# Second pointwise projection of a Conformer module, from fp32 matmuls to three products of rounded parts

## The chip, the cores and the metric

The kernel runs on one core of a Trainium2 chip. The metric is the device time of one execution in microseconds; the median of several executions is compared. The engines are TensorE (PE: matmuls; PEld: its weight loads), VectorE (DVE), ScalarE (ACT), GpSimd (POOL) and SyncE (SP), which issues most DMAs.

## The reference

A two-layer trunk over x of 256 tokens and 1024 channels, in float32. Layer 0 is a Conformer convolution module and a dense SwiGLU, layer 1 a windowed attention and a top-2-of-8 expert SwiGLU. The change lies in the convolution module:

```python
def conformer_conv_module(h, pw1_w, pw1_b, dw_w, dw_b, ln_g, ln_b, pw2_w, pw2_b):
    u = h @ pw1_w + pw1_b
    a, gate = jnp.split(u, 2, axis=-1)
    u = a * jax.nn.sigmoid(gate)
    u = lax.conv_general_dilated(u, dw_w[:, None, :], window_strides=(1,), padding=[(CONV_WIDTH - 1, 0)], ...) + dw_b
    u = jax.nn.silu(layernorm(u, ln_g, ln_b))
    return u @ pw2_w + pw2_b

x = x + conformer_conv_module(rmsnorm(x, norm_mix_g[0]), ...)
x = x + swiglu(rmsnorm(x, norm_ffn_g[0]), ffd_w_gate[0], ffd_w_up[0], ffd_w_down[0])
```

pw1_w is 1024x2048, the depthwise filter has 31 taps, pw2_w is 1024x1024.

## The kernel before

The program is written engine by engine: each engine has one instruction stream in the order of its code, and waits for semaphores that others raise. Nothing reorders the instructions. Channels stand in 8 chunks of 128 partitions (DC), tokens in two tiles of 128 (TT).

**Weights.** They come in units of 1 MB (2048 fp32 per partition) through a ring of 7 slots, which SyncE fills in order: 8 units of pw1, 4 of pw2 (U_PW2, numbers 8 to 11, each two input chunks of 1024 outputs), then 33 of the dense SwiGLU (from U_FFD, number 12), K, V, Q, the output projection and the experts. The load of unit n waits until unit n - 7 is no longer needed (L445 to L452).

**Two kinds of product.** The matmuls of pw1 (L1075), of the filter (L1095) and of pw2 (L1120) take fp32 operands as they are. From the dense SwiGLU on, each weight half-unit is split: ScalarE casts it to a rounded high part (wh, four places, L773), VectorE subtracts that from the ring's fp32 to get the low part (wl, L1611), and TensorE adds three products: high x high, high x low, low x high. Activations are split in the same manner (hTh, hTl, both in the tensor `both`).

**The convolution module.** TensorE makes pw1 in four groups of two chunks; ScalarE takes the sigmoid of each gate (L723), VectorE multiplies (L1550, the gated product). The filter is shared: VectorE makes chunks 0 to 4 and part of chunk 5 tap by tap (L1557 and 169 operations of 128x256 on L1560), TensorE the rest of 5, and 6 and 7, as 74 matmuls with diagonal matrices that ScalarE writes (L711). In VectorE's stream two gated products each stand ahead of taps number 32, 68 and 98. Then TensorE sums for mean and variance (L1085, L1106), VectorE normalizes (L1601, L1603), ScalarE applies Silu (L760) into the fp32 tensor sq, and TensorE multiplies by pw2 (L1120): tile 0, then tile 1, and for each of 8 chunks two halves of 512 outputs. After four chunks of tile 1 it transposes the updated X of tile 0 (L1021). The bias pw2_b is added to X by VectorE ahead of its first gated product (L1545), and the projection when a tile is done (add_mix, L1520). ScalarE and VectorE then write the high and low parts of the scaled X of each tile (L784, L1640), with which the dense SwiGLU begins (L1184, L1186).

GpSimd has little to do ahead of the attention: constants, powers for the norms, and the DMAs of biases and small parameters (L555 to L562).

## Time and profile before

| | |
|---|---|
| median of 3 runs | 1395.81 us (1395.0 to 1400.91) |
| profiled execution | 1393.66 us, span 1391.9 us |
| PE busy | 1370.0 us (98%) |
| DVE busy | 1178.7 us (85%) |
| ACT busy | 985.6 us (71%) |
| POOL busy | 93.3 us (7%) |
| mean granted TensorE clock | 0.997 |
| bytes moved | 428.97 MB, mean 308 GB/s |

Times in the profile count from the start of the span. Consecutive instructions of one kind are merged in the timelines: the first number is the start, the second the time from the start of the first to the end of the last, xN the count; square brackets hold the engine's idle time before the row and what ended it. Two successive instructions of one engine overlap a little in the records, so the pace is read from starts. An fp32 matmul leaves two records: the 32 instructions of L1120 show as x64. "R" stands for any of the buffers R1, R2 and R3.

### The profile page before, as it was taken

How to read it: one execution, taken by the hardware profiler on the slowest of the kernel's cores; microseconds unless marked ns; L12 is line 12 of the kernel's file. 1: busy time of each engine (PE TensorE's matmuls, PEld its weight loads, DVE VectorE, ACT ScalarE, POOL GpSimd, SP SyncE). 2: the span in 40 equal slices, each digit the busy share in tenths (PEclk: the TensorE clock that was granted, in tenths of full speed). 3: DMA queues.
4: the chain of work that ended last, by engine and by line, in shares of the span. 5: the costliest groups of instructions: out<-in, count | busy, mean ns of one | idle time of the engine just before them, and what ended most of it. 6: DMA issues, size and time to landing. Idle time of an engine off the chain costs nothing.

```text
span 1391.9 us, 20466 instructions
## 1 busy us (share of the span) xinstructions
PE 1370.0 (98%) x6699; PEld 1136.2 (82%) x6699; DVE 1178.7 (85%) x1391; ACT 985.6 (71%) x1249; POOL 93.3 (7%) x121
## 2 busy tenths in 40 slices
PE   9999999999999999999999999999999999999997
PEld 8885888888887888888888888888888888888885
DVE  3993666667768998999999899999989999999997
ACT  3174544455667788877878887787888788778885
POOL 1000000002224000000000000000000000000000
PEclk9999999999999999999999999999999999999999
DMA  9602665555637999999999999999999999999992
GB/s 293 228 24 79 205 195 187 186 198 166 197 103 289 395 396 367 395 395 374 359 394 395 337 394 394 354 376 394 393 332 394 396 353 379 395 384 342 395 394 104
DMA packets 197230, 428.97 MB, mean 308 GB/s; under 512 B 7263, under 2 KB 44255, under 8 KB 197182
## 3 DMA queue, kind: packets, MB, share of 16 engines
q1 hardware_dynamic: 192510, 412.79, 81.0%
q0 software_dynamic: 4512, 15.51, 4.0%
q8 instruction: 28, 0.46, 0.1%
q14 instruction: 20, 0.16, 0.0%
q10 hardware_dynamic: 160, 0.04, 0.0%
HBM read 419.67 MB, written 8.65 MB: 308 GB/s over the span
## 4 chain that ended last, share of the span: by engine, by line
PE 91%; DVE 4%; ACT 3%; issue 1%; ACTq 0%; DVEq 0%; POOL 0%; POOLq 0%
PE bank L1135 70%; PE bank L1184 6%; PE bank L1075 4%; PE bank L1186 3%; PE bank L1095 2%; PE bank L1120 2%; PE bank L1424 2%; DVE wl L1611 2%; ACT wh L773 1%; PE bank L1001 1%; ACT prob L853 0%; ACT both L916 0%; PE bank L1106 0%; PE bank L1332 0%; PE bank L1085 0%
## 5 line engine op out<-in xcount | busy, mean ns | idle before, releaser
L1611 DVE TENSOR_TENSOR wl<-ring,wh 128x1024 fp32r<-128x1024 f32 x758 | 907.9, 1224 | 70.7 <-ACT wh L773 25.7
L773 ACT CAST wh<-ring 128x1024 fp32r<-128x1024 f32 x758 | 789.3, 1055 | 167.5 <-PE bank L1135 167.5
L1135 PE MATMUL bank<-wh,both 128*128 128x512 f32 (+1 forms) x1888 | 583.5, 391 | 0.9 <-DVE wl L1611 0.7
L1135 PEld LDWEIGHTS bank<-wh,both 128*128 128x128 f32 x1888 | 349.0, 188 | 72.3 <-DVE wl L1611 2.8
L1135 PE MATMUL bank<-wl,both 128*128 128x512 f32 (+1 forms) x944 | 366.4, 388 | 0.0
L1135 PEld LDWEIGHTS bank<-wl,both 128*128 128x128 f32 x944 | 177.2, 188 | 37.1
L1135 PE MATMUL bank<-wh,ath 128*128 128x512 f32 x512 | 201.2, 393 | 0.9
L1135 PE MATMUL bank<-wl,ath 128*128 128x512 f32 x512 | 199.6, 390 | 0.0
L1135 PE MATMUL bank<-wh,atl 128*128 128x512 f32 x512 | 199.3, 389 | 0.0
L1184 PE MATMUL bank<-both,wh 128*128 128x512 f32 x352 | 124.8, 399 | 1.4 <-DVE both L1640 1.1
L1135 PEld LDWEIGHTS bank<-wh,ath 128*128 128x128 f32 x512 | 96.1, 188 | 23.5 <-DVE wl L1611 3.8
L1135 PEld LDWEIGHTS bank<-wl,ath 128*128 128x128 f32 x512 | 96.1, 188 | 20.6
L1135 PEld LDWEIGHTS bank<-wh,atl 128*128 128x128 f32 x512 | 96.2, 188 | 19.4
L1186 PE MATMUL bank<-both,wl 128*128 128x256 f32 x352 | 98.7, 280 | 0.0
L1184 PEld LDWEIGHTS bank<-both,wh 128*128 128x128 f32 x352 | 66.1, 188 | 18.1 <-DVE both L1640 1.4
L1560 DVE SCALAR_TENSOR_TENSOR R<-R 128x256 f32<-128x256 f32 x169 | 67.5, 500 | 0.0
L1186 PEld LDWEIGHTS bank<-both,wl 128*128 128x128 f32 x352 | 66.4, 189 | 0.4
L1075 PE MATMUL bank<-R,ring 128*128 128x256 f32 x256 | 55.8, 380 | 0.1
L1075 PEld LDWEIGHTS bank<-R,ring 128*128 128x128 f32 x256 | 48.5, 190 | 7.1 <-issue 0.6
L1890 DVE TENSOR_TENSOR atl<-bank,ath 128x512 fp32r<-128x512 f32 x56 | 38.4, 686 | 10.5 <-ACT ath L931 10.5
L931 ACT CAST ath<-bank 128x512 fp32r<-128x512 f32 x56 | 32.4, 579 | 16.8 <-PE bank L1424 16.8
L1897 DVE TENSOR_TENSOR R<-bank,R 128x512 f32<-128x512 f32 x56 | 38.3, 685 | 1.8 <-PE bank L1135 1.8
(251 smaller groups left out, 892.0 us busy)
## 6 DMA issues: line engine op xcount, KB each, us to landing
ring<-in_moe_w_gate SPq DMA_DIRECT2D x112, 1024.0 KB, 7.4
ring<-in_moe_w_up SPq DMA_DIRECT2D x112, 1024.0 KB, 7.7
ring<-in_moe_w_down SPq DMA_DIRECT2D x112, 1024.0 KB, 7.8
ring<-in_conv_pw_w SPq DMA_DIRECT2D x12, 1024.0 KB, 10.9
ring<-in_ffd_w_gate SPq DMA_DIRECT2D x11, 1024.0 KB, 5.3
ring<-in_ffd_w_up SPq DMA_DIRECT2D x11, 1024.0 KB, 5.5
ring<-in_ffd_w_down SPq DMA_DIRECT2D x11, 1024.0 KB, 5.0
ring<-in_w_q SPq DMA_DIRECT2D x4, 1024.0 KB, 4.9
```

What stands on the lines that cost most here:

```text
L773: sa.copy(wh[:, place(n, h), :], ring_half(n, h)).then_inc(wh_ready, 1)
L931: sa.copy(ath[:, :, :], PB[2][:, :].rearrange("p (j s) -> p j s", j=4)).then_inc(ath_ready, 1)
L1075: mm = pe.matmul(PB[2 * g + j % 2][:, c * S:(c + 1) * S], w[:, k, c * P:(c + 1) * P], hT[:, k, :], start=(k == 0), stop=(k == DC - 1))
L1095: mm = pe.matmul(PB[4 + c - DVE_CHUNKS][:, 0:S], taps[:, m % DIAGS, :], upad[:, c, w:w + S], start=(w == 0), stop=(w == last_tap))
L1120: mm = pe.matmul(x_bank(t, half)[:, :], tokens(sq[:, k, :], t), w[:, k % 2, half * HALF:(half + 1) * HALF], start=(k == 0), stop=(k == DC ...
L1135: mm = pe.matmul(out_bank, lhs, rhs, start=start and n == 0, stop=stop and n == 2, **kw)
L1184: pe.matmul(banks[c][:, :], wide, hTb[:, k, :, :].rearrange("p a s -> p (a s)"), start=(k == 0), stop=False)
L1186: mm = pe.matmul(banks[c][:, 0:S], narrow, hTh[:, k, :], start=False, stop=(k == DC - 1))
L1560: ins = ve.scalar_tensor_tensor(out=v, in0=upad[:, c, w:w + S], scalar=dw[:, c, w:w + 1], in1=v, op0=ALU.mult, op1=ALU.add)
L1611: ve.tensor_tensor(wl[:, place(n, h), :], ring_half(n, h), wh[:, place(n, h), :].bitcast(F32), ALU.subtract).then_inc(wl_ready, 1)
L1890: ve.tensor_tensor(atl[:, :, :], PB[2][:, :].rearrange("p (j s) -> p j s", j=4), ath[:, :, :].bitcast(F32), ALU.subtract).then_inc(atl_rea ...
L1897: ve.tensor_tensor(act, PB[1][:, :], act, ALU.mult).then_inc(act_ready, 1)
```

## The change

1. The second projection is made of three products of rounded parts. The eight half-units of pw2 get high parts (mix_high: the four places of wh, and hnl, yh and yl, which have no other use until much later) and low parts (mix_low: the four places of wl, and qh and ql).
2. ScalarE casts the high parts behind the sigmoids of chunks 3 and 5, four each. GpSimd subtracts for the low parts, each when its high part is ready.
3. ScalarE applies Silu twice, once into the rounded hTh and once into the fp32 sq; VectorE's mix_lows subtract, to hTl.
4. SyncE reloads the ring slots of pw2 when the low parts exist, no longer when the matmuls are done. The first four feed-forward casts wait for the chunks of tile 1 that still use their places.
5. The bias pw2_b is added to X by GpSimd instead of VectorE.
6. VectorE's small preparations (router weights, sinks) and the first feed-forward low parts stand behind the mix_lows and the addition of tile 0 to X.

```diff
--- before.py
+++ after.py
@@ -180,6 +180,10 @@
         hTb = both[:, CHUNK:CHUNK + 2 * DC * S].rearrange("p (k a s) -> p k a s", k=DC, a=2)
         hTh, hTl = hTb[:, :, 0, :], hTb[:, :, 1, :]
 
+        mix_high = [wh[:, k, :] for k in range(SPLITS)] + [hnl[:, 0, :], hnl[:, 1, :], yh[:, :], yl[:, :]]
+        mix_low = [wl[:, k, :] for k in range(SPLITS)] + [q.rearrange("p (c k) s -> p c (k s)", c=2)[:, c, :]
+                                                          for q in (qh, ql) for c in range(2)]
+
         upad = R2[:, :].rearrange("p (k s) -> p k s", k=DC)
         sq = R2[:, 0:2048].rearrange("p (k s) -> p k s", k=DC)
         dw = R3[:, 2816:3072].rearrange("p (k w) -> p k w", k=DC)
@@ -295,6 +299,10 @@
         std_ready = sem("std_ready")
         vn_ready = sem("vn_ready")
         s_ready = sem("s_ready")
+        s_high = sem("s_high")
+        s_low = sem("s_low")
+        mix_high_ready = sem("mix_high_ready")
+        mix_low_ready = sem("mix_low_ready")
         tile_done = sem("tile_done")
         x_upd = sem("x_upd")
         dve = sem("dve_chain")
@@ -445,7 +453,9 @@
             def load(n, src, k):
                 if n >= RING:
 
-                    if n - RING < U_FFD:
+                    if U_PW2 <= n - RING < U_FFD:
+                        sp.wait_ge(mix_low_ready, 2 * (n - RING - U_PW2 + 1))
+                    elif n - RING < U_FFD:
                         sp.wait_ge(units_used, n - RING + 1)
                     else:
                         split_done(sp, n - RING, 1)
@@ -562,6 +572,16 @@
             pool.dma_start(scratch, spread(small[0:HEADS, 0:DELTAS].rearrange("h (a d) -> h a d", a=1), 1, CHUNK))\
                 .then_inc(bias_out, 16)
 
+            pool.wait_ge(pw2b_in, 16)
+            pool.wait_ge(xT_done, 4)
+            for t in range(TT):
+                pool.tensor_tensor(X[:, t, :], X[:, t, :], pw2_bias, ALU.add).then_inc(x_biased, 1)
+
+            for k in range(DC):
+                pool.wait_ge(mix_high_ready, k + 1)
+                pool.tensor_tensor(mix_low[k], ring_half(U_PW2 + k // 2, k % 2), mix_high[k].bitcast(F32),
+                                   ALU.subtract).then_inc(mix_low_ready, 1)
+
             for t in range(TT):
                 root(1, t)
 
@@ -722,6 +742,12 @@
                     sa.wait_ge(glu_ready, c - 1)
                 sa.activation(sig[:, c % 2, :], PB[2 + c // 2 % 2][:, (c % 2) * S:(c % 2 + 1) * S], ACT.Sigmoid,
                               bias=cv[:, CV_PW1B + DC + c:CV_PW1B + DC + c + 1]).then_inc(sig_ready, 1)
+                if c in (3, 5):
+
+                    for k in range(2 * c - 6, 2 * c - 2):
+                        if k % 2 == 0:
+                            landed(sa, U_PW2 + k // 2)
+                        sa.copy(mix_high[k], ring_half(U_PW2 + k // 2, k % 2)).then_inc(mix_high_ready, 1)
 
             def taps_to(c):
 
@@ -757,9 +783,9 @@
                 for c in range(DC):
 
                     sa.wait_ge(vn_ready, 2 * t + (1 if c < DVE_CHUNKS else 2))
-                    sa.activation(tokens(sq[:, c, :], t), tokens(v_chunk(c), t), ACT.Silu,
-                                  bias=cv[:, CV_LNB + c:CV_LNB + c + 1],
-                                  scale=cv[:, CV_LNG + c:CV_LNG + c + 1]).then_inc(s_ready, 1)
+                    norm = dict(bias=cv[:, CV_LNB + c:CV_LNB + c + 1], scale=cv[:, CV_LNG + c:CV_LNG + c + 1])
+                    sa.activation(tokens(hTh[:, c, :], t), tokens(v_chunk(c), t), ACT.Silu, **norm).then_inc(s_high, 1)
+                    sa.activation(tokens(sq[:, c, :], t), tokens(v_chunk(c), t), ACT.Silu, **norm).then_inc(s_ready, 1)
 
 
             def high_parts(n, later=0):
@@ -768,6 +794,9 @@
                     if n >= U_MOE or half_no(n, h) >= SPLITS:
 
                         sa.wait_ge(halves_used, later * PASS_HALVES + (half_no(n, h) - SPLITS + 1))
+                    elif h == 0:
+
+                        sa.wait_ge(units_used, U_PW2 + half_no(n, h) // 2 + 1)
                     if h == 0:
                         landed(sa, n, later)
                     sa.copy(wh[:, place(n, h), :], ring_half(n, h)).then_inc(wh_ready, 1)
@@ -1112,14 +1141,17 @@
                 for k in range(DC):
                     if t == 1 and k == 4:
                         raw_T(1, 0, xT_first)
-                    if t == 0 and k % 2 == 0:
-                        landed(pe, U_PW2 + k // 2)
-                    pe.wait_ge(s_ready, DC * t + k + 1)
-                    w = slot(U_PW2 + k // 2).rearrange("p (k f) -> p k f", k=2)
-                    for half in range(2):
-                        mm = pe.matmul(x_bank(t, half)[:, :], tokens(sq[:, k, :], t),
-                                       w[:, k % 2, half * HALF:(half + 1) * HALF], start=(k == 0),
-                                       stop=(k == DC - 1))
+                    if t == 0:
+                        pe.wait_ge(mix_low_ready, k + 1)
+                    pe.wait_ge(s_high, DC * t + k + 1)
+                    for a, w in ((hTh, mix_high[k]), (hTh, mix_low[k]), (hTl, mix_high[k])):
+                        if a is hTl:
+                            pe.wait_ge(s_low, DC * t + k + 1)
+                        for half in range(2):
+                            mm = pe.matmul(x_bank(t, half)[:, :], tokens(a[:, k, :], t),
+                                           w[:, half * HALF:(half + 1) * HALF],
+                                           start=(k == 0 and a is hTh and w is mix_high[k]),
+                                           stop=(k == DC - 1 and a is hTl))
                     if t == TT - 1 and k % 2:
                         consume(mm)
                 if t == 0:
@@ -1539,10 +1571,6 @@
             ve.wait_ge(bias_row_done, 1)
             ve.tensor_copy(bias_rows, PB[1][0:HEADS, 0:DELTAS]).then_inc(bias_row, 1)
 
-            ve.wait_ge(pw2b_in, 16)
-            ve.wait_ge(xT_done, 4)
-            for t in range(TT):
-                ve.tensor_tensor(X[:, t, :], X[:, t, :], pw2_bias, ALU.add).then_inc(x_biased, 1)
             ve.wait_ge(cv_ready, 2)
 
             def glu(c):
@@ -1623,6 +1651,17 @@
                                             in1=high_part[:, k, :].bitcast(F32), op0=ALU.mult,
                                             op1=ALU.subtract).then_inc(h_low, 1)
 
+            def mix_lows(t, chunks):
+
+                for c in chunks:
+                    ve.wait_ge(s_ready, DC * t + c + 1)
+                    ve.tensor_tensor(tokens(hTl[:, c, :], t), tokens(sq[:, c, :], t),
+                                     tokens(hTh[:, c, :], t).bitcast(F32), ALU.subtract).then_inc(s_low, 1)
+
+            mix_lows(0, range(DC))
+            mix_lows(1, range(DC))
+            ve.wait_ge(x_biased, 2)
+            add_mix(1, 0)
             ve.wait_ge(router_in, 32)
             ve.tensor_tensor(rw[:, :, :], rw[:, :, :],
                              spread(cv[:, CV_FFN1:CV_FFN1 + DC].rearrange("p (k a) -> p k a", a=1), 2, E),
@@ -1631,7 +1670,6 @@
             ve.tensor_scalar(nsinks[:, :], sinks[:, :], -1.0, None, ALU.mult).then_inc(nsinks_ready, 1)
             low_parts(dense_at["g", 0])
             low_parts(dense_at["u", 0])
-            ve.wait_ge(x_biased, 2)
             def norm_low_tile(t):
                 for k in range(DC):
                     if k % 2 == 0:
@@ -1642,7 +1680,6 @@
                                             in1=tokens(hTh[:, k, :], t).bitcast(F32), op0=ALU.mult,
                                             op1=ALU.subtract).then_inc(h_low, 1)
 
-            add_mix(1, 0)
             mean_square(1, 0)
             scale_diag(1, 0)
             norm_low_tile(0)
```

TensorE at the second projection, before (ring is the fp32 weight slot, R the activations sq):

```order
L1001 MATMUL bank<-ident 128x128 x10
L1120 MATMUL bank<-ring,R 128x512 x24
L1021 MATMUL bank<-ident,X 128x128 x8
L1120 MATMUL bank<-ring,R 128x512 x8
L1001 MATMUL bank<-ident 128x128 x2
L1021 MATMUL bank<-ident,X 128x128 x8
```

The same place now: the first chunks of tile 0, the transposes within tile 1, the end of tile 1 (L1151 is the projection; wl, qh and ql hold low parts of weights, wh, hnl, yh and yl high ones):

```order
L1030 MATMUL bank<-ident 128x128 x10
L1151 MATMUL bank<-wh,both 128x512 x2
L1151 MATMUL bank<-wl,both 128x512 x2
L1151 MATMUL bank<-wh,both 128x512 x4
L1151 MATMUL bank<-wl,both 128x512 x2
...
L1151 MATMUL bank<-wl,both 128x512 x2
L1151 MATMUL bank<-wh,both 128x512 x2
L1050 MATMUL bank<-ident,X 128x128 x8
L1151 MATMUL bank<-hnl,both 128x512 x2
...
L1151 MATMUL bank<-ql,both 128x512 x2
L1151 MATMUL bank<-yl,both 128x512 x2
L1030 MATMUL bank<-ident 128x128 x2
L1050 MATMUL bank<-ident,X 128x128 x8
```

Each fp32 matmul gives way to three on parts, 96 in all; the transposes keep their place after four chunks of tile 1.

GpSimd between its early DMAs and the LayerNorm, before:

```order
L559 DMA gB<-in_norm_ffn_g 128x1024
L562 DMA bias_scratch<-small 1024x1x192
L548 TENSOR_TENSOR rstd<-ms,mhalf 128x1 x2
L569 MEMSET ones 128x128
L548 TENSOR_TENSOR rstd<-ms,mhalf 128x1 x2
```

The same place now (L578 adds the bias, L582 makes the low parts of the eight half-units of pw2):

```order
L569 DMA gB<-in_norm_ffn_g 128x1024
L572 DMA bias_scratch<-small 1024x1x192
L578 TENSOR_TENSOR X<-X,R 128x1024 x2
L582 TENSOR_TENSOR wl<-ring,wh 128x1024 x4
L582 TENSOR_TENSOR qh<-ring,hnl 128x1024 x2
L582 TENSOR_TENSOR ql<-ring,yh 128x1024
L582 TENSOR_TENSOR ql<-ring,yl 128x1024
L558 TENSOR_TENSOR rstd<-ms,mhalf 128x1 x2
```

Ten operations of 128x1024 stand where there was none.

VectorE at the start of the filter, and behind the LayerNorm, before (L1545 adds the bias, L1603 is the last LayerNorm product, L1611 the first feed-forward low parts, L1520 the addition of tile 0):

```order
L1545 TENSOR_TENSOR X<-X,R 128x1024 x2
L1550 SCALAR_TENSOR_TENSOR R<-bank,cv,R 128x256 x2
L1557 TENSOR_SCALAR R<-R,cv 128x256 x2
L1560 SCALAR_TENSOR_TENSOR R<-R 128x256 x30
...
L1603 TENSOR_TENSOR R<-R 128x3x128
L1627 TENSOR_TENSOR rw<-rw,cv 128x64
L1631 TENSOR_SCALAR nsinks<-sinks 128x16
L1611 TENSOR_TENSOR wl<-ring,wh 128x1024 x4
L1520 TENSOR_TENSOR X<-bank,X 128x512 x2
```

The same two places now:

```order
L1578 SCALAR_TENSOR_TENSOR R<-bank,cv,R 128x256 x2
L1585 TENSOR_SCALAR R<-R,cv 128x256 x2
L1588 SCALAR_TENSOR_TENSOR R<-R 128x256 x30
...
L1631 TENSOR_TENSOR R<-R 128x3x128
L1658 TENSOR_TENSOR both<-R,both 128x128 x16
L1552 TENSOR_TENSOR X<-bank,X 128x512 x2
L1666 TENSOR_TENSOR rw<-rw,cv 128x64
L1670 TENSOR_SCALAR nsinks<-sinks 128x16
L1639 TENSOR_TENSOR wl<-ring,wh 128x1024 x4
```

The bias is gone from the head of the filter; 16 low parts of activations (L1658) and the addition of tile 0 (L1552) stand ahead of the feed-forward low parts (L1639).

## Rows read from the trace of the kernel before

**Rows 1.** The page, part 4: shares of the chain that ended last, by engine

```profile
PE 91%; DVE 4%; ACT 3%; issue 1%; ACTq 0%; DVEq 0%; POOL 0%; POOLq 0%
```

**Rows 2.** The chain in order of time, 0 to 160 us: start, length, what

```profile
66.97 30.23 PE bank L1095 x140
...
101.08 1.29 PE bank L1085 x6
...
110.63 20.84 PE bank L1120 x48
...
132.34 6.88 PE bank L1120 x16
139.25 0.70 DVE X L1520
```

**Rows 3.** Waits of the DMA queue (SPq), whole run: waited for, total us, times, longest

```profile
SPq L507 <- DVE wl L1611: 821.7, 336, 21.6
```

**Rows 4.** Timeline of VectorE, 25 to 101 us: start us, us, what, count

```profile
25.93 2.36 DVE L1545 TENSOR_TENSOR X<-X,R 128x1024 f32<-128x1024 f32 x2 [7.12 <-DMA R<-in_conv_pw_b]
...
29.76 11.98 DVE L1560 SCALAR_TENSOR_TENSOR R<-R 128x256 f32<-128x256 f32 x30
41.63 0.89 DVE L1550 SCALAR_TENSOR_TENSOR R<-bank,cv,R 128x256 f32<-128x256 f32 x2
...
69.11 0.89 DVE L1550 SCALAR_TENSOR_TENSOR R<-bank,cv,R 128x256 f32<-128x256 f32 x2
...
95.62 4.47 DVE L1560 SCALAR_TENSOR_TENSOR R<-R 128x256 f32<-128x256 f32 x11
```

**Rows 5.** Timeline of ScalarE: two of the four pairs of sigmoids

```profile
39.38 0.84 ACT L723 ACTIVATE R<-bank,cv 128x256 f32<-128x256 f32 x2 [10.64 <-PE bank L1075]
...
67.00 0.84 ACT L723 ACTIVATE R<-bank,cv 128x256 f32<-128x256 f32 x2 [12.98 <-PE bank L1075]
```

**Rows 6.** Groups by line and form, 0 to 210 us: count, busy us, mean ns, idle

```profile
L1120 PE MATMUL bank<-ring,R 128*128 128x512 f32 x64 | 27.9, 593 | 0.2 <-ACT R L760 0.2
...
L773 ACT CAST wh<-ring 128x1024 fp32r<-128x1024 f32 x26 | 25.9, 1054 | 0.0
...
L760 ACT ACTIVATE R<-R,cv 128x128 f32<-128x128 f32 x16 | 6.2, 478 | 0.0
```

**Rows 7.** Timeline of TensorE in the experts, 610 to 614 us

```profile
611.51 0.62 PE L1135 MATMUL bank<-wh,both 128*128 128x512 f32 x2
...
613.57 0.62 PE L1135 MATMUL bank<-wh,both 128*128 128x512 f32 x2
```

**Rows 8.** Timelines of ScalarE and VectorE in the second tile

```profile
126.03 1.06 ACT L685 ACTIVATE R<-X 128x1024 f32<-128x1024 f32 x1 [6.00 <-DVE X L1520]
...
128.06 0.29 DVE L1503 TENSOR_SCALAR R<-ident,rstd 128x128 f32<-128x128 f32 x1 [0.69 <-POOL rstd L548]
...
132.38 2.16 DVE L1640 SCALAR_TENSOR_TENSOR both<-bank,cv,both 128x128 fp32r<-128x128 f32 x8 [4.04 <-ACT both L784]
```

**Rows 9.** Groups by form on GpSimd, 360 to 430 us

```profile
L617 POOL TENSOR_TENSOR prob<-X,gB 128x1024 f32<-128x1024 f32 x2 | 4.8, 2403 | 12.9 <-DVE X L1520 12.9
```

**Rows 10.** Timelines from 419 us (GpSimd, VectorE); by tile: ns min/median/max

```profile
419.89 7.54 POOL L633 TENSOR_SCALAR prob<-prob,rstd 128x1024 f32<-128x1024 f32 x2
...
422.73 4.70 POOL L633 TENSOR_SCALAR prob<-prob,rstd 128x1024 f32<-128x1024 f32 x1
...
424.70 3.20 DVE L1611 TENSOR_TENSOR wl<-ring,wh 128x1024 fp32r<-128x1024 f32 x2
...
L1611 DVE TENSOR_TENSOR wl<-ring,wh x11: 1214/1217/2056, 422.4 to 438.9; 128x1024 fp32r<-128x1024 f32 x11
```

**Rows 11.** Timelines of GpSimd and VectorE from 364 us

```profile
364.22 2.04 POOL L606 TENSOR_TENSOR prob<-prob,small 128x512 f32<-128x512 f32 x2 [14.90 <-DVE small L1754]
...
364.19 1.66 DVE L1739 SCALAR_TENSOR_TENSOR prob<-bank,rstd,bias 128x256 f32<-128x256 f32 x4
```

**Rows 12.** Stretch table: us, busy (count) PE PEld DVE ACT POOL, PEclk, DMA, GB/s

```profile
412.00:415.40 3.40, 3.40 (x19) 3.40 (x18) 3.08 (x13) 1.13 (x2) 0.00 (x0) 0.50 0.01 2
```

## The prediction

> **What bounds the kernel now.** I read the chain of work that ended last first: TensorE holds 91% of it [rows 1]. So something counts only where TensorE waits or where its own work gets shorter. The chain in order of time shows the stretch of the change [rows 2]: up to 97 us TensorE goes from the first projection into the depthwise filter without a wait (70 taps in 30.23 us, 0.432 us each), at 101.08 it starts the last three sums for the LayerNorm mean, and the second projection runs from 110.63 to 139.2, as 24 matmuls in 20.84 us and 8 in 6.88: 27.7 us for 32. VectorE is the second bound. Its tap chain (0.40 us each: 30 in 11.98) has no gap from 25.93 until 95.62 + 4.47 = 100.1 us [rows 4], about 1 us before TensorE would need it. Behind the projection the weight stream never bounds: the DMA queue waits 821.7 us for weights to be split, thus for room [rows 3]. A microsecond won or lost before 142 us is kept to the end.
>
> **The matmuls.** 32 fp32 matmuls (0.866 us each) become 96 on rounded parts. Steady three-product matmuls of the same 512 columns start at 611.51 and 613.57 with nine between: 0.229 us each [rows 7]. 96 x 0.229 = 22.0 us, 5.7 less than 27.7. Bounds: a quarter of 0.866 (0.217) gives 20.8 us, 0.24 would give 23.0. Feeding: ScalarE now computes Silu twice per chunk and tile, 32 instead of 16 at 0.39 [rows 6], so 110.0 to 122.5 us; TensorE needs a chunk's pair per 1.37 us and gets it per 0.78. VectorE's 16 low parts (nearest row: eight of 128x128 in 2.16 us, 0.27 each [rows 8]) follow in the same pace; only the first is late, by an estimated 0.2 us, since VectorE is still at the LayerNorm products. Tile 0 ends at 110.6 + 11.0 + 0.2 = 121.8 us.
>
> **The second tile's tail.** VectorE adds tile 0 to X at 122.8 to 124.1, after the last low part; TensorE wants it for its transposes only at 127.3, half into tile 1: no wait. But the first feed-forward casts (four, 1.055 us each [rows 6]), which stood at 116 to 120 us in cover, now write into the places of the projection's high parts and wait for chunks 1 and 3 of tile 1: 124.6 and 127.3. They end at 129.4. Behind them on ScalarE stand the square and the eight scaled high parts of tile 0, and behind those on VectorE the diagonal and the lows. From square to diagonal it takes 126.03 to 128.35 now [rows 8], so 129.4 to 131.8, and eight lows end near 134.2. Only then comes the addition of tile 1, for which TensorE's own work (121.8 + 5.5 + 1.0 + 5.5) would be ready at 133.9. It starts at 134.3 where it starts at 139.25 now [rows 2]: **4.9 us gained**, 0.8 lost to this queue.
>
> **Work that I cost at nothing.** The eight casts of projection weights on ScalarE (8 x 1.055 = 8.4 us) stand behind the sigmoids of 39.4 and 53.2 us, where ScalarE idles for over 10 us until the next pair (the wait is printed in [rows 5]); the last weights are requested when unit 4 is used up, one unit (16 x 0.432 = 6.9 us) ahead of the sigmoids of 53.2. If they landed so late that the casts ran into the sigmoids of 67.0, VectorE's chain would pay. Four ring slots come free at about 50 to 65 us instead of during tile 1, so SyncE's next four loads go out at 67 us behind its wait for unit 7, into a DMA that is nearly idle then; nobody waits for them now either. The bias addition leaves VectorE (2.36 us [rows 4]): its chain starts when sigmoid 1 is there, 2.16 us sooner, reaches its 32nd tap at 39.5, where sigmoid 3 lets it go on at about 39.9 [rows 5], and sigmoid 7 at 67.8 holds it again. TensorE is busy all that time, so this is slack, not time.
>
> **GpSimd beside the taps.** Here lies the doubt. GpSimd gets ten two-input operations of 128x1024: 2 for the bias from 25.9 us, 8 low parts between about 42 and 69 us. One takes 2.40 us [rows 9]: 24 us in all, done long before 110. The question is what they do to the taps, which read two SBUF tensors each. Where VectorE read one SBUF tensor and PSUM, four operations took 1.66 us beside a GpSimd product (0.415 each, as the taps' 0.40) [rows 11]: nothing lost. The one place where both engines read SBUF, VectorE with two tensors, is [rows 10]: the first GpSimd scaling took 7.54 - 4.70 = 2.84 us, the second, beside the weight lows, 4.70; and one low took 2.056 us where 1.217 is the median. So GpSimd waited 1.86 us and VectorE lost 0.84 us to one 128x1024 operation. Call H what VectorE loses per operation. Below nothing is excluded (GpSimd gives VectorE no work). The ends are 0 and 2.40 (its whole length); I take 0.84, since that row is nearest in kind and size, though it reads one tensor and ours two.
>
> The first bias operation falls beside the gated products, which read PSUM; the second costs H. VectorE's 32nd tap is then at 39.5 + H; from there 27.5 us as now (41.63 to 69.11) plus 8H, then 31.0 us to the end: 98.0 + 9H. TensorE's taps end at 101.1 and two of the last three mean sums need VectorE's last chunks, so up to about 101.5 is free. The path grows by 9H - 3.5: at 0.84 by **4.1 us**. Sum: -4.9 + 4.1 = **-0.8 us**. The profiled execution took 1393.66 us (span 1391.9), so 1392.9; the median of the runs lies 2.15 above it, so the forecast for a median is 1395.0 us. A measurement of this kernel can tell about 0.5% (7 us) from no change: this is none.
>
> **Rivals.**
> 1. GpSimd and the taps don't hinder each other (H up to 0.4): -4.9 us, 1390.9; with the 0.217 matmul -6.1. For it: GpSimd's products beside one-tensor operations [rows 11], and taps leave a third of their 0.40 us without elements to read. Against: [rows 10]. Chance 0.22.
> 2. H grows with the tensors that GpSimd reads: 2 x 0.84 = 1.68. The taps end at 113.1, the path grows by 11.6: +6.7 us, 1402.5. TensorE would then stand for some 10 us at chunk 6, whose gated product comes at 82; the only stretch at half the clock so far [rows 12] followed work of 8-column matmuls, so an idle engine may well get 1.2 GHz behind it, and each tap at that level costs 0.43 us more. Chance 0.20.
> 3. **The slower side**: GpSimd holds VectorE for its whole 2.40 us. Place: the tap chain from 28 to 69 us. 9 x 2.40 - 3.5 = 18.1, net +13.2 us, 1409.0. It costs anything from H = 0.39, and the kernel is slower than before from H = 0.93. Against it: in [rows 10] the low that began at 424.70 ended at 426.76, while GpSimd ran on until 427.43. Chance 0.13.
> 4. GpSimd doesn't get in between back-to-back taps, and its operations start when VectorE is done at 98. Ten times 2.40 from there puts the last low part at 122, and tile 0 ends at about 123.5 instead of 121.8: net about -3 us. Also the case in which the split isn't hidden as the change says. Chance 0.05.
>
> The Trainium skill (SBUF — State Buffer, "Who interferes with whom") states the third as a rule: VectorE with two SBUF inputs and a GpSimd instruction that reads SBUF share one read interface, as an exclusive lock held for the whole instruction. By that rule the time would be the 1409.0 of rival 3. This trace agrees that both engines wait (1.86 and 0.84 us), but not with the length of the hold, and it has one such place only.
>
> **How the numbers follow.** The forecast case, H between 0.4 and 1.3, spans -4.8 to +3.3 us and has 0.40. With rivals 1 and 4, the lower part of rival 2 and all of the forecast case the time stays within 0.5%: 0.64. Faster by over 0.5% (below 1388.8) needs rival 1, the quickest matmuls and one microsecond more: 0.08. Slower (above 1402.8) are half of rival 2, rival 3, and 0.05 for a stall that costs the clock too: 0.28. The range goes from rival 1 with the 0.217 matmul, less a little (1389.0), to H of 2.1 (+10.5 us: 1406.5); it leaves out rival 3 and a bit below.
>
> **What would show it.** Right: the 96 matmuls start every 0.229 us and span some 22 us; VectorE adds tile 1 to X 23.7 us after the first matmul of the projection, where it takes 28.6 now; taps that overlap GpSimd show up to 0.84 us more, a dozen of them, and GpSimd's lows take 3 us or more instead of 2.4; TensorE has one wait of 3 to 4 us, at chunk 6 of the filter. Wrong: VectorE's last tap at 99 us (rival 1) or later than 112 (rivals 2 and 3); GpSimd's lows standing after 100 us (rival 4); a matmul above 0.24 us; ScalarE's casts running into the sigmoids at 67 us; a tail wait in tile 1 of more than 1 us.

## The result and the profile after

The changed kernel takes **1407.2 us** (median of 10 runs, 1404.11 to 1415.13); the kernel before has 1395.8 us beside it (10 runs). The ratio is 1.0082, 95% interval 1.0063 to 1.0101: **11.4 us slower**. The forecast was 1395.0 us, range 1389.0 to 1406.5, with 0.28 for slower. The profiled execution takes 1405.07 us, span 1403.3.

The chain that ended last, first by engine (the page's part 4, answering to [rows 1]), then in order of time (start, length, what; answering to [rows 2]):

```profile
PE 86%; DVE 8%; ACT 3%; issue 1%; POOL 1%; ACTq 0%; DMA 0%; DVEq 0%; POOLq 0%
```

```profile
27.20 3.80 DVE R L1585 x2
...
55.54 4.74 DVE R L1585 x2
60.28 9.94 DVE R L1588 x4
...
86.75 27.43 PE bank L1124 x116
118.07 1.29 PE bank L1114 x6
...
127.62 16.78 PE bank L1151 x72
...
144.42 1.06 ACT wh L802
...
145.50 2.36 DVE wl L1639 x2
...
148.90 2.07 DVE both L1678 x8
150.97 0.61 DVE X L1552
...
154.00 0.50 PE bank L1216
```

VectorE's share has doubled, and it stands there with the taps from 27 us on: four taps in 9.94 us where four take 1.6 without GpSimd. The last mean sums start at 118.07 instead of 101.08: **17.0 us lost**. From the first projection matmul to the addition of tile 1 it is 23.35 us instead of 28.62: **5.3 us gained**. Together +11.7 us at the addition (150.97 against 139.25), and +11.4 at the end of the span (1403.3 against 1391.9): nothing behind this stretch adds to the loss.

Where the taps lose it: GpSimd's low parts and VectorE in the timelines (start, length of one, what; before, these taps ran at 0.40 us each, [rows 4]):

```profile
44.41 13.37 POOL L582 TENSOR_TENSOR wl<-ring,wh 128x1024 fp32r<-128x1024 f32 x1 [13.56 <-ACT wh L750]
57.73 2.40 POOL L582 TENSOR_TENSOR wl<-ring,wh 128x1024 fp32r<-128x1024 f32 x1
...
62.45 2.52 POOL L582 TENSOR_TENSOR wl<-ring,wh 128x1024 fp32r<-128x1024 f32 x1
64.94 2.52 POOL L582 TENSOR_TENSOR qh<-ring,hnl 128x1024 fp32r<-128x1024 f32 x1
```

```profile
28.56 2.44 DVE L1585 TENSOR_SCALAR R<-R,cv 128x256 f32<-128x256 f32 x1
...
43.59 11.95 DVE L1588 SCALAR_TENSOR_TENSOR R<-R 128x256 f32<-128x256 f32 x30
...
55.46 2.46 DVE L1585 TENSOR_SCALAR R<-R,cv 128x256 f32<-128x256 f32 x1
57.84 2.43 DVE L1585 TENSOR_SCALAR R<-R,cv 128x256 f32<-128x256 f32 x1
60.20 2.57 DVE L1588 SCALAR_TENSOR_TENSOR R<-R 128x256 f32<-128x256 f32 x1
62.69 2.57 DVE L1588 SCALAR_TENSOR_TENSOR R<-R 128x256 f32<-128x256 f32 x1
...
70.14 0.47 DVE L1578 SCALAR_TENSOR_TENSOR R<-bank,cv,R 128x256 f32<-128x256 f32 x1
```

Three things are to be seen. The record of GpSimd's first low part (L582) starts at 44.41 and lasts 13.37 us: through the 30 taps that run on undisturbed (11.95 us), until the one-tensor TENSOR_SCALAR at 55.46. From there the engines take turns, **one VectorE operation per GpSimd operation**: a tap starts every 2.49 us instead of every 0.40, a loss of 2.1 us each. From the first of the 30 taps to the last tap it is 86.2 us (30.92 to 117.08), before the change 70.3 (29.76 to 100.09): the eight low parts cost 15.8 us, 2.0 each on average. And the gated products at 70.14, which read PSUM and one SBUF tensor, take 0.47 us in the same traffic.

TensorE's waits between 66 and 96 us, and the stretch table (columns as in [rows 12]):

```profile
PE bank L1124 <- DVE R L1578: 12.8, 2, 8.8
```

```profile
79.00:87.00 8.00, 0.25 (x1) 0.28 (x2) 8.00 (x22) 0.00 (x0) 0.00 (x0) 0.62 0.57 180
87.00:92.00 5.00, 5.00 (x15) 4.02 (x16) 5.00 (x13) 2.25 (x6) 0.00 (x0) 0.59 0.01 3
92.00:100.00 8.00, 8.00 (x39) 7.00 (x38) 8.00 (x22) 7.43 (x20) 0.00 (x0) 1.00 0.00 0
```

TensorE waits 12.8 us for gated products, 4 of them at chunk 5 and 8.8 at chunk 6, and its granted clock is 0.62 in the wait at chunk 6 and 0.59 in the first 5 us behind it: near the lower level, 1.2 GHz (0.50), before it is back at 1.00.

### The profile page after: what moved, and what is told of

Its sections match the earlier page's. It is cut to its first block, busy times and chain, and to the rows that moved or that the text cites. A ratio compares the mean times of both kernels' runs of the same rounds, so it can differ in the third digit from the quotient of the medians.

```text
span 1403.3 us, 20584 instructions
## 1 busy us (share of the span) xinstructions
PE 1367.6 (97%) x6731; PEld 1142.8 (81%) x6731; DVE 1199.9 (86%) x1405; ACT 1000.9 (71%) x1273; POOL 129.6 (9%) x131
## 4 chain that ended last, share of the span: by engine, by line
PE 86%; DVE 8%; ACT 3%; issue 1%; POOL 1%; ACTq 0%; DMA 0%; DVEq 0%; POOLq 0%
PE bank L1167 70%; PE bank L1216 6%; DVE R L1588 3%; PE bank L1218 3%; PE bank L1124 2%; PE bank L1456 2%; DVE wl L1639 2%; PE bank L1151 1%; ACT wh L802 1%; PE bank L1104 1%; DVE R L1585 1%; ACT both L945 0%; POOL prob L626 0%; PE bank L1135 0%; DMA bias<-bias_scratch 0%
## 5 line engine op out<-in xcount | busy, mean ns | idle before, releaser
L1639 DVE TENSOR_TENSOR wl<-ring,wh 128x1024 fp32r<-128x1024 f32 x758 | 907.9, 1224 | 66.8 <-ACT wh L802 22.0
L1588 DVE SCALAR_TENSOR_TENSOR R<-R 128x256 f32<-128x256 f32 x169 | 79.1, 543 | 0.0
L1124 PE MATMUL bank<-R,prob 128*128 128x256 f32 x148 | 36.2, 408 | 12.8 <-DVE R L1578 12.8
L1124 PEld LDWEIGHTS bank<-R,prob 128*128 128x128 f32 x148 | 30.4, 207 | 18.4 <-issue 13.6
```

Of the source, the lines that this page charges most:

```text
L1124: mm = pe.matmul(PB[4 + c - DVE_CHUNKS][:, 0:S], taps[:, m % DIAGS, :], upad[:, c, w:w + S], start=(w == 0), stop=(w == last_tap))
L1588: ins = ve.scalar_tensor_tensor(out=v, in0=upad[:, c, w:w + S], scalar=dw[:, c, w:w + 1], in1=v, op0=ALU.mult, op1=ALU.add)
L1639: ve.tensor_tensor(wl[:, place(n, h), :], ring_half(n, h), wh[:, place(n, h), :].bitcast(F32), ALU.subtract).then_inc(wl_ready, 1)
```

## Experiments

All edits are against the changed kernel. Each time has the kernel before beside it on the same chip: its median was 1394.05 us beside e1 to e4, 1394.16 beside e5 to e8, 1393.86 beside e9 and e10, 1394.53 beside e11, and 1395.8 beside the changed kernel. So the ratios are to be compared, not the medians. "Last tap" is the end of VectorE's last tap, "addition" the start of the addition of tile 1 to X; both are from one profiled execution, and the executions differ already in when the first gated product starts (26.1 to 26.9 us where the bias is not ahead of it on VectorE).

| run | last tap, us | addition, us | median, us | ratio to before (95%) |
|---|---|---|---|---|
| before | 100.09 | 139.25 | 1395.8 | 1 |
| changed | 117.08 | 150.97 | 1407.2 | 1.0082 (1.0063 to 1.0101) |
| e1 bias on VectorE | 116.65 | 150.43 | 1404.09 | 1.0073 (1.0056 to 1.0089) |
| e2 memsets | 102.97 | 135.77 | 1389.65 | 0.9972 (0.9956 to 0.9987) |
| e3 copies | 106.82 | 141.27 | 1516.06 | not comparable, see below |
| e4 quarters | 115.44 | 149.26 | 1403.95 | 1.0076 (1.0059 to 1.0093) |
| e5 lows on VectorE, behind | 98.64 | 134.17 | 1389.0 | 0.9956 (0.9941 to 0.9971) |
| e6 filler, too long | 116.94 | 156.76 | 1413.01 | 1.0129 (1.0113 to 1.0146) |
| e7 lows on GpSimd, behind | 100.72 | 145.38 | 1400.75 | 1.0037 (1.0024 to 1.0051) |
| e8 lows on VectorE, among taps | 110.06 | 143.76 | 1400.46 | 1.0037 (1.0026 to 1.0048) |
| e9 filler, mended | 117.12 | 149.92 | 1405.35 | 1.008 (1.0063 to 1.0097) |
| e10 one small operation | 117.04 | 150.89 | 1405.19 | one run, no ratio |
| e11 products with 0 | 106.01 | 140.26 | 1392.85 | 0.9987 (0.9976 to 0.9997) |

### What holds the taps: e1 to e4

**e1**: is it the bias?

```diff
-            for t in range(TT):
-                pool.tensor_tensor(X[:, t, :], X[:, t, :], pw2_bias, ALU.add).then_inc(x_biased, 1)
...
+            for t in range(TT):
+                ve.tensor_tensor(X[:, t, :], X[:, t, :], pw2_bias, ALU.add).then_inc(x_biased, 1)
```

> Only the bias goes back to VectorE, ahead of its first gated product; GpSimd keeps the eight low parts. Theory (a GpSimd operation that reads SBUF holds VectorE for its whole length, once each): the bias cost VectorE about 3 us of hold and saved it 2.2, so the 30 taps start at 29.8 instead of 30.9, the last tap ends near 116 instead of 117.1, and the time falls by about 1 us, to 1406. Rival (the bias operations, at the head of the chain, are what throws the chain off): the last tap ends below 110, time below 1400.

The last tap ends 0.4 us sooner. Here the bias addition itself began 0.7 us later than before the change (26.63 against 25.93), so the bias on GpSimd costs some 1.1 us at most, and the intervals of the two ratios overlap: the bias is not the loss.

**e2**: GpSimd only writes. The low parts of the weights are left out (zeros), so the sum is the same number of matmuls on less.

```diff
-                pool.tensor_tensor(mix_low[k], ring_half(U_PW2 + k // 2, k % 2), mix_high[k].bitcast(F32),
-                                   ALU.subtract).then_inc(mix_low_ready, 1)
+                pool.memset(mix_low[k].bitcast(F32), 0.0).then_inc(mix_low_ready, 1)
```

> GpSimd's eight subtractions become eight memsets of the same 128x1024 places, which write SBUF and read nothing (the low parts of the weights are left out of the product). Theory (the hold is on the shared read side): no tap is delayed, the last one ends at 99 to 101 us, the projection starts near 111, and the time is 1390 to 1392. Rival (any GpSimd operation on SBUF beside the taps holds VectorE): eight taps of over 1 us, last tap after 105, time above 1396.

VectorE's last tap ends 14.1 us sooner, and the time is 1389.65: the low parts' share of the loss, with everything else of the change in place. At 102.97 it is later than the 99 to 101 expected: the first gated product started 0.6 us later than in the changed kernel (26.93), the bias is still on GpSimd, and 1.2 us come from what the expectation did not have. A memset takes 0.95 us and leaves two-tensor taps alone, but not the two one-tensor TENSOR_SCALARs:

```profile
56.02 1.92 DVE L1584 TENSOR_SCALAR R<-R,cv 128x256 f32<-128x256 f32 x2
```

They take 1.92 us where 0.72 is usual, while the four taps behind them, beside two memsets, take their usual 1.66. The Trainium skill (SBUF — State Buffer, "Who interferes with whom") has both halves: a VectorE instruction with two SBUF inputs contends only with a GpSimd instruction that reads SBUF, and tensor_scalar can, when its operands meet the conditions, enter a mode that takes the shared pair of ports whole. This trace agrees with the first by the 1.66 us, and with the second only so far as that the two TENSOR_SCALARs are late; no run shows in which mode they ran.

**e3**: GpSimd reads one tensor, in a copy. The low parts are then whole weights, so the values are others, more weights are split than in the changed kernel (842 low parts on VectorE against 758), and only the stretch of the filter can be read; the total of 1516.06 us means nothing.

```diff
-                pool.tensor_tensor(mix_low[k], ring_half(U_PW2 + k // 2, k % 2), mix_high[k].bitcast(F32),
-                                   ALU.subtract).then_inc(mix_low_ready, 1)
+                pool.tensor_copy(mix_low[k], ring_half(U_PW2 + k // 2, k % 2)).then_inc(mix_low_ready, 1)
```

> GpSimd's eight subtractions become eight copies of the ring's half-units (one SBUF tensor read instead of two; the products are then of the whole weights rounded and not of low parts). Theory (VectorE is held for the operation's whole length): delayed taps last as long as one copy does, whatever that is; if a copy takes 1.2 us, the eight cost about 8 us and the last tap ends near 107, time 1396 to 1399. Rival (held for the reads at line rate, 0.84 us a tensor): the taps lose 0.84 us each even where the copy takes longer, last tap near 105.

```profile
57.80 4.78 DVE L1587 SCALAR_TENSOR_TENSOR R<-R 128x256 f32<-128x256 f32 x4
```

A copy takes 1.09 to 1.23 us, and held taps follow each other every 1.18 us: a loss of 0.78 each. The last tap ends at 106.82, as the theory of the whole length said for this duration (near 107).

**e4**: each subtraction in four pieces of 128x256.

```diff
-                pool.tensor_tensor(mix_low[k], ring_half(U_PW2 + k // 2, k % 2), mix_high[k].bitcast(F32),
-                                   ALU.subtract).then_inc(mix_low_ready, 1)
+                for q in range(4):
+                    cols = slice(q * S, (q + 1) * S)
+                    ins = pool.tensor_tensor(mix_low[k][:, cols], ring_half(U_PW2 + k // 2, k % 2)[:, cols],
+                                             mix_high[k][:, cols].bitcast(F32), ALU.subtract)
+                ins.then_inc(mix_low_ready, 1)
```

> Each of GpSimd's eight subtractions is cut into four of 128x256. Theory (whole length, one VectorE operation gets in between two GpSimd operations): 32 taps of some 0.7 us plus start cost instead of eight of 2.5; the sum of the holds stays the same or grows by up to 4 us, last tap at 117 to 121, time 1406 to 1411. Rival (a hold has a fixed cost each, or short operations fit into the gaps of the taps): the last tap ends before 112 and the time is below 1402.

```profile
56.85 3.55 DVE L1591 SCALAR_TENSOR_TENSOR R<-R 128x256 f32<-128x256 f32 x4
```

A piece comes every 0.87 us and lets one tap through, a loss of 0.47. The last tap ends at 115.44, between what the theory (117 to 121) and the rival (before 112) said: neither had the size. 32 pieces cost 14.3 us from the first of the 30 taps to the last, where eight whole subtractions cost 15.8. What counts is how much GpSimd subtracts, little in how many operations.

### Why the row of before said 0.84 us: e11

The forecast took its hold from [rows 10], where GpSimd multiplied one tensor by a scalar. Here the subtractions give way to the same kind of operation (low parts left out, as in e2):

```diff
-                pool.tensor_tensor(mix_low[k], ring_half(U_PW2 + k // 2, k % 2), mix_high[k].bitcast(F32),
-                                   ALU.subtract).then_inc(mix_low_ready, 1)
+                pool.tensor_scalar(mix_low[k], ring_half(U_PW2 + k // 2, k % 2), 0.0, None,
+                                   ALU.mult).then_inc(mix_low_ready, 1)
```

> The changed kernel, with each of GpSimd's eight subtractions replaced by a product of the ring's half-unit with the constant 0: one tensor read, as in [rows 10], same size. The low parts of the weights are left out. It asks why the hold in [rows 10] was 0.84 us and not the operation's whole length. If the product takes L alone (2.84 in [rows 10] with a scalar per partition), theory 'any GpSimd operation that reads SBUF holds the taps for its whole length': held taps follow each other every L + 0.1 us, the loss is L - 0.4 each, and with L = 2.8 the last tap ends near 119 us, the time near 1407; with L = 1.2, as the copy of e3, near 107 us and 1394. Rival 'a product with one tensor holds only a part, as [rows 10] showed': the taps go on 0.75 us before GpSimd's record ends, the last tap with L = 2.8 at 113 or less, the time at 1401 or less.

GpSimd and VectorE in the timelines of e11:

```profile
60.95 2.79 POOL L582 TENSOR_SCALAR wl<-ring 128x1024 fp32r<-128x1024 f32 x1
63.71 2.79 POOL L582 TENSOR_SCALAR wl<-ring 128x1024 fp32r<-128x1024 f32 x1
```

```profile
60.24 0.86 DVE L1588 SCALAR_TENSOR_TENSOR R<-R 128x256 f32<-128x256 f32 x2
...
61.03 1.25 DVE L1588 SCALAR_TENSOR_TENSOR R<-R 128x256 f32<-128x256 f32 x1
62.21 0.87 DVE L1588 SCALAR_TENSOR_TENSOR R<-R 128x256 f32<-128x256 f32 x2
```

The product runs from 60.95 to 63.74, but only the tap at 61.03 is held: the next follows after 1.18 us, at 62.21, and more at the full pace while GpSimd still works. The loss is 1.18 - 0.40 = 0.78 us, next to the 0.84 of [rows 10]. The rival named in the expectation holds, and the rule "for the whole length" fails for this kind.

The last tap ends at 106.01, and the forecast's own formula with 0.84 gave 98.0 + 9 x 0.84 = 105.6, but that they lie so close is in part luck. The eight products cost 4.9 us in all (30.78 to 106.01 against 70.3 us before), not 6.7, since some of them meet operations that lose less or nothing; the two bias additions still read two tensors each and hold VectorE's TENSOR_SCALARs for 3 us, not 0.84. The time is 1392.85 us, 1.7 below the kernel before beside it, though in the profiled execution (1397.01 us, the longest of the nine) the addition comes 1.0 us later than before. Side by side, for 128x1024: nothing read, 0 us lost to a two-tensor tap; one tensor read, 0.78 whether the operation lasts 1.2 (copy) or 2.8 us (product); two tensors read, 2.1 of 2.4 us. The operation changes with the number of tensors (memset; copy and product; subtraction), so that the number itself is the cause is likely, not shown.

### What lets GpSimd in: e10

```diff
+                if m == 50:
+                    ve.tensor_scalar(nsinks[:, :], ident[:, 0:HEADS], -1.0, None, ALU.mult)
```

> The changed kernel, with one 128x16 operation with one tensor input on VectorE ahead of tap 50, in the middle of the second undisturbed run of 30 taps. Theory 'two-tensor operations back to back keep the port and one operation of another kind lets GpSimd in': the small operation comes at about 48 us, GpSimd's first low starts to run there (record of some 6 us instead of 13.37), the taps behind it are held one by one from there on, and the eight lows end near 65 instead of 74.9; the sum of holds stays the same (8 x 2.1), so the last tap stays at about 117 and the time at 1407. Rival 'GpSimd is let in only when VectorE waits, or after a fixed time': the first low still takes some 13 us and its end stays at 57.8.

VectorE and GpSimd around the added operation:

```profile
43.44 7.20 DVE L1588 SCALAR_TENSOR_TENSOR R<-R 128x256 f32<-128x256 f32 x18
50.56 2.32 DVE L1600 TENSOR_SCALAR nsinks<-ident 128x16 f32<-128x16 f32 x1
52.80 4.83 DVE L1588 SCALAR_TENSOR_TENSOR R<-R 128x256 f32<-128x256 f32 x12
57.55 4.80 DVE L1585 TENSOR_SCALAR R<-R,cv 128x256 f32<-128x256 f32 x2
```

```profile
44.38 8.47 POOL L582 TENSOR_TENSOR wl<-ring,wh 128x1024 fp32r<-128x1024 f32 x1 [13.67 <-ACT wh L750]
52.81 7.03 POOL L582 TENSOR_TENSOR wl<-ring,wh 128x1024 fp32r<-128x1024 f32 x1
```

The first low now ends at 52.85, right with the small operation, which takes 2.32 us for 16 columns. But the next 12 taps then run undisturbed, with the second low waiting, until the next TENSOR_SCALAR at 57.55; I had expected turns from there. The sum of holds is the same, and so is the last tap (117.04). So one operation with one tensor lets one GpSimd operation in. It is not the only way in: behind the two TENSOR_SCALARs the subtractions get in between two taps, here as in the changed kernel (60.20 to 70 us there), and in e11 so do products. What decides between these cases is open.

### The place of the low parts: e7, e8, e5

**e7** keeps the low parts on GpSimd, behind VectorE's last tap (bias on VectorE, as in e1):

```diff
+            pool.wait_ge(v_dve, DVE_CHUNKS + 1)
             for k in range(DC):
                 pool.wait_ge(mix_high_ready, k + 1)
```

> GpSimd keeps the eight low parts but starts them when VectorE's last tap is done; the bias is back with VectorE at the head of the chain. Theory (each GpSimd operation holds one VectorE operation that reads two SBUF tensors for up to 2.1 us): the taps end at 100 to 101 us as before the change, GpSimd runs without a break until about 122, some four LayerNorm products and then low parts of activations are held, and the loss is 5 to 10 us in place of 17: time 1394 to 1400. Rival (behind the filter nothing is held, since VectorE is often idle there): 1390 to 1392.

VectorE's LayerNorm, and TensorE's waits:

```profile
108.55 2.27 DVE L1630 TENSOR_TENSOR R<-R 128x640 f32<-128x640 f32 x1
110.73 2.72 DVE L1632 TENSOR_TENSOR R<-R 128x384 f32<-128x384 f32 x1
```

```profile
PE bank L1148 <- ACT both L784: 9.1, 2, 8.7
PEld bank L1148 <- DVE both L1659: 9.2, 1, 9.2
```

The taps are free, but the LayerNorm products read two SBUF tensors too, and take 2.27 and 2.72 us instead of 0.82 and 0.55. The first low part of an activation is held as well:

```profile
118.89 2.43 DVE L1659 TENSOR_TENSOR both<-R,both 128x128 fp32r<-128x128 f32 x1
```

TensorE stands 8.7 us in the projection, until 121.37. For the matmul the profile names ScalarE, for its weight load this low part (L1659), which ends at 121.32 and which the third pair of matmuls needs. The conflict moves with the operations. The time, 1400.75 us, is just above the 1394 to 1400 expected, and the rival (1390 to 1392) is out.

**e8** gives the same subtractions to VectorE, four ahead of tap 68 and four ahead of tap 98 (bias stays on GpSimd):

```diff
+                for k in {68: range(4), 98: range(4, DC)}.get(m, ()):
+                    weight_low(k)
```

> VectorE itself makes the eight low parts, four each ahead of the taps at which GpSimd got in (taps 68 and 98); GpSimd keeps the bias. Theory (GpSimd's 2.5 us operation costs VectorE 2.1 us, its own subtraction 1.15): VectorE spends 9.2 us instead of losing some 17; the last tap ends near 108 us instead of 117.1, and the time is 1397 to 1399. Rival (the loss has another cause than the hold, such as TensorE's waits for the gated products): no gain over the changed kernel, 1405 or more.

```profile
57.44 4.62 DVE L1592 TENSOR_TENSOR wl<-ring,wh 128x1024 fp32r<-128x1024 f32 x4
```

VectorE does four in 4.62 us, 1.15 each. It is cheaper for VectorE to make a low part (1.15) than to be held by GpSimd making it (2.1). The last tap ends 7.0 us sooner than in the changed kernel; still TensorE waits 7.6 us at chunk 6, and the result is slower than before. The last tap (110.06 against 108) and the time (1400.46 against 1397 to 1399) are later than expected; the eight subtractions themselves cost the 9.1 us foreseen, and the bias, which GpSimd kept, may be the rest.

**e5** puts them where TensorE doesn't wait for VectorE: three behind the last tap, one ahead of the reciprocals, four between the low parts of the activations; the bias stands on VectorE behind tile 0's. GpSimd has none of it.

```diff
+            for k in range(3):
+                weight_low(k)
             ve.wait_ge(mean_done, 1)
...
+            weight_low(3)
             for t in range(TT):
                 ve.wait_ge(std_ready, t + 1)
...
-            mix_lows(0, range(DC))
+            for c in range(DC):
+                mix_lows(0, (c,))
+                if c + 4 < DC:
+                    weight_low(c + 4)
```

> The eight low parts of the weights go to VectorE, behind its taps: three before the mean, one before the reciprocals, four between the low parts of the activations; the bias also to VectorE, behind tile 0's low parts. GpSimd does nothing beside the filter. Theory (what the change lost is the hold of the taps alone, and the three products are worth 5 us): the last tap ends near 98 us, the projection starts within 1 us of where it did before the change and takes 16.8 + 5.5 us, the addition of tile 1 comes 4 to 5 us sooner than before; time 1389 to 1392, ratio to before 0.996. Rival (four subtractions between the activations' low parts starve TensorE): waits on low parts of over 3 us in tile 0, time above 1394.

```profile
98.56 3.49 DVE L1612 TENSOR_TENSOR wl<-ring,wh 128x1024 fp32r<-128x1024 f32 x3
...
104.98 1.22 DVE L1612 TENSOR_TENSOR wl<-ring,wh 128x1024 fp32r<-128x1024 f32 x1
...
111.59 1.22 DVE L1612 TENSOR_TENSOR qh<-ring,hnl 128x1024 fp32r<-128x1024 f32 x1
```

The addition comes at 134.17, 5.1 us ahead of before, with no wait of TensorE over 1.1 us between 60 and 140 us. The time is 1389.0 us, the ratio 0.9956 (0.9941 to 0.9971): **faster than both kernels**, 0.4% below the one before. The change's idea was sound; the engine for the low parts was not.

### What the clock costs: e6 and e9

Both put matmuls without use on TensorE where it waits for the gated products of chunks 5 and 6.

```diff
                 if w == 0:
+                    keep_busy(7, {5: 16, 6: 36}.get(c, 0))
                     pe.wait_ge(glu_ready, c + 1)
```

e6 had 32 and 70 there:

> The changed kernel with 102 matmuls of 128x128 on the identity put where TensorE waits for the gated products of chunks 5 and 6, so that it isn't idle there. Theory (VectorE's chain sets the end of the filter; the lower clock after the wait only eats slack of TensorE): the granted clock stays at 1.0 from 66 to 92 us, TensorE's taps are done 2 to 4 us sooner, but the projection starts less than 1 us sooner, time 1406 to 1407. Rival (the idle clock is what costs): the projection starts 3 us sooner, time 1403 to 1404.

The 70 took 15.79 us, since one takes 0.226 us and not half of that, as I had reckoned from its records. TensorE came back to the taps at 94.78 instead of 86.75, so the run's 1413.01 us tell nothing on its question. e9 is the mended form:

> The changed kernel, with 16 and 36 transposing-size matmuls (128x128, fp32, 0.226 us each as the filler of e6 ran) on TensorE where it stands idle for 4.05 us at chunk 5 and 8.76 us at chunk 6 of the filter. They should end just before the gated products come, so that only the clock differs. Theory 'the delayed gated products are all, the clock adds a little': TensorE's taps behind 86.75 us run at 0.432 us from the first instead of four at 0.85, its last tap comes 1.5 to 2 us sooner (about 116.4 instead of 118.1), but the projection then waits for VectorE's last tap at 117.1, which nothing moves; gain 0 to 1.5 us, 1405.7 to 1407.2. Rival 'the clock is a large part of the loss': gain of 3 us or more, 1404 or less.

```profile
76.36 8.20 PE L1030 MATMUL bank<-ident 128*128 128x128 f32 x72
86.69 25.32 PE L1125 MATMUL bank<-R,prob 128*128 128x256 f32 x116 [2.13 <-DVE R L1579]
```

The granted clock is 1.00 from 66 to 127 us, the taps from 86.7 on take 25.32 instead of 27.43 us for the same records, and the projection starts at 126.59 instead of 127.62, where VectorE's last tap sets it. So of the 11.7 us **the clock is 1.0**, by one profiled execution of each; the total of 1405.35 us (ratio 1.008) is not to be told from the changed kernel's.

## Why the prediction was wrong

**The step that failed** is the size of H: "I take 0.84, since that row is nearest in kind and size, though it reads one tensor and ours two". It measured 2.1, from the starts of held taps. e11 shows that the row was read rightly and carried to the wrong kind: with the row's operation in its place the loss is 0.78 and the kernel is 1.7 us faster than before (forecast: 0.8), not 11.4 slower. The doubt in the half-sentence should have decided the number.

**The frame held.** With H = 2.1 the formula gives 98.0 + 9 x 2.1 = 116.9 for the last tap (117.08 measured). The path grows by 9 x 2.1 - 3.5 = 15.4, the rest gains 4.9, the clock, which the sum had at nothing, takes 1.0: +11.5 us, against 11.4 to 11.7 measured. So good an agreement is in part luck. The eight low parts cost 2.0 each on average and the bias hold was 3.1 us, not one H, which cancels; and without the clock the path grew by 16.0 and the rest gained 5.3, 0.6 and 0.4 more than the formula says, in opposite directions. The forecast's range did reach to H = 2.1 (1406.5 us); the clock lay beyond it.

**The matmuls** come every 0.227 to 0.231 us (forecast 0.229), with no wait but 0.2 us for the first pair. From the first to the addition of tile 1 it is 23.35 us (forecast 23.7). The queue of casts stands in the chain behind 144.42 as described, but it goes on through the feed-forward low parts on VectorE (145.50, 2.36 us), which the forecast did not name.

**What was costed at nothing** cost little. The casts stand at 43.28 to 47.8 and 54.06 to 57.9 us, ahead of the next sigmoids; SyncE's loads went out from 67.14 on; the bias on GpSimd holds VectorE's two TENSOR_SCALARs for 3 us at 27 to 31, most of which the earlier start gives back: e1 puts 0.4 to 1.1 us of it at the last tap.

**The rivals.** Rival 3, the hold of the whole length, gave 1409.0 us and was right for the subtractions: 2.49 us between held taps, where the operation itself takes 2.40 alone. Its price was too high by the tap's own 0.40: held for 2.5 us, a tap loses 2.1, not 2.40. The Trainium skill (SBUF — State Buffer, "Who interferes with whom") calls the shared pair of ports an exclusive lock; it spells out "for the whole instruction" beside VectorE's two-port modes, and the prediction took it for the lock in general. So read, the rule agrees with the trace for the subtractions. It does not in e11, where a product of 2.79 us holds for 1.18. Rival 2 had the right dependence, on the tensors read, as far as the runs tell, but doubled the loss (1.68) where 2.7 times was right (2.1 over 0.78). Its second half, TensorE idle at chunk 6 and at the lower clock behind it, came true (8.8 us, 1.0 us). Rival 4 was right in that back-to-back taps keep GpSimd out, for 13.37 us, but a one-tensor operation ends this, long before 98. Rival 1 is out: the last tap ended at 117.08, not at 99. The chances were off too: rival 3 had 0.13, against a forecast on one row of another kind.

## What to carry to other kernels

GpSimd is no free engine beside VectorE: before work moves to it, count the SBUF tensors that both engines' operations read. Here a 128x1024 subtraction on GpSimd cost VectorE more (2.1 us) than doing it itself (1.15 us), so it belonged on VectorE, at a place where nobody waits for VectorE. And a hold read from one row may be carried only to the same kind of operation: a product of 2.8 us with one tensor cost less than a subtraction of 2.4 us with two, so the duration of the record does not give it.

## What was not expected of the hardware

- VectorE's two-tensor operations back to back kept a waiting GpSimd subtraction out for 11 us (44.41 to 55.4); one VectorE operation of 128x16 with one tensor let it in (e10).
- Once a subtraction was in, the engines took turns one for one: a tap of 0.40 us per subtraction of 2.4 us, and one per quarter of it at 0.87 us (e4). Behind a single TENSOR_SCALAR they did not (e10); what decides is open.
- A GpSimd product of 128x1024 holds a two-tensor VectorE operation for 1.18 of its 2.79 us (e11), at its start.
- A GpSimd memset leaves two-tensor taps alone and delays one-tensor operations: 1.92 us for two, where 0.72 is usual (e2).
